# First weight loads in half units, tile order in two mixers, and gate rows made by transposes, in a twelve-step transformer kernel

## The reference

```python
def modulate(x, g, shift, scale):
    return rms_norm(x, g) * (1.0 + scale) + shift

def macaron_half_ffn(x, g, shift, scale, gate, w_in, w_out):
    return x + 0.5 * gate * swiglu_2(modulate(x, g, shift, scale), w_in, w_out)
```

## Time and profile before

| | |
|---|---|
| median of 3 runs | 3711.2 us (3710.67 to 3714.84) |
| span of the profiled execution | 3705.4 us |
| TensorE busy | 3626.4 us (98%), 18926 matmuls |
| VectorE, ScalarE, GpSimd busy | 2313.8, 1524.9, 273.7 us |
| loads by SP, and by GpSimd | 579.22 MB, 78.56 MB |
| chain that ended last, by engine | PE 91%, DVE 5%, ACT 3%, DMA 1%, issue 1% |

### The profile page before, as it was taken

How to read it: one execution, slowest core, us unless ns; L and a number is a source line. 1 busy time by engine, 2 the same in 40 slices (tenths; PEclk the granted TensorE clock), 3 DMA queues, 4 the chain that set the end, 5 groups by cost and what they waited for, 6 DMA issues and landing times.

```text
span 3705.4 us, 48300 instructions
## 1 busy us (share of the span) xinstructions
PE 3626.4 (98%) x18926; PEld 3031.7 (82%) x18926; DVE 2313.8 (62%) x3018; ACT 1524.9 (41%) x2001; POOL 273.7 (7%) x322
## 2 busy tenths in 40 slices
PE   8999999999999999999999999999999999999999
PEld 7898788889788875888898788888888588889887
DVE  6767577774577755777777576555434555555654
ACT  4454244443434424444463344444311444444443
POOL 0003200000000001000004100000000200000000
PEclk9999999999999999999999999999999999999999
DMA  9652177664476744676641384555521355454452
GB/s 317 228 160 86 59 244 242 239 216 153 165 255 204 261 147 145 236 241 224 219 160 37 120 275 167 204 170 195 175 79 53 118 179 196 170 181 155 171 185 99
DMA packets 453679, 660.58 MB, mean 178 GB/s; under 512 B 15305, under 2 KB 385444, under 8 KB 453049
## 3 DMA queue, kind: packets, MB, share of 16 engines
q1 hardware_dynamic: 431970, 579.22, 46.0%
q0 software_dynamic: 21072, 78.56, 6.6%
q10 hardware_dynamic: 454, 0.26, 0.0%
HBM read 656.94 MB, written 2.00 MB: 178 GB/s over the span
## 4 chain that ended last, share of the span: by engine, by line
PE 91%; DVE 5%; ACT 3%; issue 1%; DMA 1%; POOL 0%; ACTq 0%; SPq 0%; POOLq 0%; DVEq 0%
PE ps L813 14%; PE ps L815 14%; PE ps L814 14%; PE ps L833 7%; PE ps L835 7%; PE ps L834 7%; PE ps L3260 3%; PE ps L1160 2%; PE ps L823 2%; PE ps L1579 2%; DVE parts L750 1%; PE ps L507 1%; PE ps L509 1%; PE ps L508 1%; PE ps L3257 1%; ACT parts L736 1%
## 5 line engine op out<-in xcount | busy, mean ns | idle before, releaser
L750 DVE TENSOR_TENSOR parts<-ring,parts 128x2048 fp32r<-128x2048 f32 (+1 forms) x339 | 756.9, 2234 | 575.1 <-ACT parts L736 575.1
L813 PE MATMUL ps<-parts 128*128 128x512 f32 x2288 | 906.3, 396 | 0.5 <-DVE parts L1020 0.5
L815 PE MATMUL ps<-parts 128*128 128x512 f32 x2288 | 892.9, 390 | 0.0
L814 PE MATMUL ps<-parts 128*128 128x512 f32 x2288 | 892.0, 390 | 0.0
L736 ACT ACTIVATE parts<-ring 128x2048 fp32r<-128x2048 f32 x346 | 661.3, 1913 | 543.6 <-PE ps L815 421.4
L815 PEld LDWEIGHTS ps<-parts 128*128 128x128 f32 x2288 | 429.7, 188 | 91.0
L813 PEld LDWEIGHTS ps<-parts 128*128 128x128 f32 x2288 | 430.2, 188 | 85.9 <-issue 1.7
L814 PEld LDWEIGHTS ps<-parts 128*128 128x128 f32 x2288 | 430.5, 188 | 84.5
L833 PE MATMUL ps<-parts 128*128 128x512 f32 x1144 | 451.0, 394 | 0.7 <-DVE parts L757 0.5
L835 PE MATMUL ps<-parts 128*128 128x512 f32 x1144 | 446.6, 390 | 0.0
L834 PE MATMUL ps<-parts 128*128 128x512 f32 x1144 | 445.8, 390 | 0.0
(11 more groups left out here) (444 smaller groups left out, 4591.0 us busy)
## 6 DMA issues: line engine op xcount, KB each, us to landing
ring<-in_ffn_w_gu SPq DMA_DIRECT2D x176, 1024.0 KB
ring<-in_ffn_w_in SPq DMA_DIRECT2D x110, 1024.0 KB
ring<-in_ffn_w_down SPq DMA_DIRECT2D x88, 1024.0 KB
ring<-in_ffn_w_out SPq DMA_DIRECT2D x55, 1024.0 KB
ring<-in_gdn_w_in SPq DMA_DIRECT2D x32, 1024.0 KB
arena<-in_w_mod POOLq DMA_DIRECT2D x24, 1024.0 KB, 5.9
xn<-in_w_mod POOLq DMA_DIRECT2D x24, 1024.0 KB, 7.5
arena<-in_w_mod POOLq DMA_DIRECT2D x48, 512.0 KB, 9.0
```

Of the source, the lines that this page charges most:

```text
L750: ins = nc.vector.tensor_tensor(lower, unit_raw(at, j)[:, sides_, :], upper, ALU.subtract)
L813: nc.tensor.matmul(dst, h_u, w_u[:, :, n, :], start=(k == 0), stop=False)
L814: nc.tensor.matmul(dst, h_u, w_l[:, :, n, :], start=False, stop=False)
L815: ins = nc.tensor.matmul(dst, h_l, w_u[:, :, n, :], start=False, stop=(k == KD - 1))
```

## The change

- **First loads.** x comes in two DMAs, one for each row tile, each with its own semaphore. The gate and up weights of load 0 come as four DMAs of 0.5 MB instead of two of 1 MB: first the two that make unit 0, then the two that make unit 1, with one semaphore for each unit; the output weights raise the slot's semaphore by 48 alone. Three semaphores that were used once are shared with later uses, whose counts are raised.
- **First step.** ScalarE squares all four quarters, casts unit 0, casts the four quarters, casts unit 1. VectorE splits unit 0 ahead of the quarters of tile 0, and unit 1 ahead of `rows_dve`. TensorE's order becomes: transposes of tile 0, spin, `up(0,0,0)`, transposes of tile 1, `up(0,0,1)`, `rows_pe`, `up(0,1,0)`, `up(0,1,1)`.
- **sb and sgu.** The first four products are unit 0 tile 0, unit 1 tile 0, unit 0 tile 1, unit 1 tile 1. `unit_freed` follows: the buffer of unit 0 is free after the third product (it was the second), that of unit 1 after the fourth.
- **Gate rows.** The broadcasts in `gate_pe` and `weigh` are transposes instead of fp32 products.

```diff
@@ ffn_load
+        if it is None and g == 0:
+            for half in range(2):
+                ks = slice(half * KD // 2, (half + 1) * KD // 2)
+                for side in range(2):
+                    sp.dma_start(part(g, side).rearrange("p (k f) -> p k f", k=KD)[:, ks, :],
+                                 gu_v[:, ks, side * FF:side * FF + CH]).then_inc(first_units[half], 16)
+            sp.dma_start(part(g, 2).rearrange("p (j d) -> p j d", d=D), down_v[0]).then_inc(load_done[s], 48)
+            return
@@ unit_freed
-        first = at["kind"] in ("ffn", "gdn") and j < 2 and at is not PLACES[0]
+        first = at["kind"] in ("ffn", "gdn", "sb", "sgu") and j < 2 and at is not PLACES[0]
         return 2 * at["unit"] + (3 + j if first else 2 * j + 2)
@@ gu_upper_act
-        if j == 0 or g != unit_load(at, j - 1):
+        if at is PLACES[0] and j < GU_SLOTS:
+            act.wait_ge(first_units[j], 32)
+        elif j == 0 or g != unit_load(at, j - 1):
@@ down_upper_act
+        if g == 0 and j == 0:
+            act.wait_ge(load_done[0], 48)
@@ ffn_pe
-        early = at is PLACES[0] or at["n"] in (CTX_FFN, CTX_FFN + 1)
+        early = at["n"] in (CTX_FFN, CTX_FFN + 1)
...
-        if early:
+        if at is PLACES[0]:
+            spin(9, 3)
+        elif early:
             norm_pe(pe, at, 1)
-            if at is PLACES[0]:
-                rows_pe(pe)
-                spin(9, 3)
-            elif at["n"] == CTX_FFN:
+            if at["n"] == CTX_FFN:
...
         up(0, 0, 0)
-        if not early:
+        if at is PLACES[0] or not early:
             norm_pe(pe, at, 1)
         for half, t in ((0, 1), (1, 0), (1, 1)) if at is PLACES[0] else ((1, 0), (0, 1), (1, 1)):
             up(0, half, t)
+            if at is PLACES[0] and (half, t) == (0, 1):
+                rows_pe(pe)
@@ ffn_act
-        if at["n"] >= 8:
+        if at["n"] >= 8 or at is PLACES[0]:
             square_act(act, at, NQ - 1, 0, src)
+        if at is PLACES[0]:
+            gu_upper_act(act, at, 0)
...
         if at is PLACES[0]:
-            for j in range(GU_SLOTS):
-                gu_upper_act(act, at, j)
+            gu_upper_act(act, at, 1)
             rows_act(act)
@@ ffn_dve
         def lower_rows(t):
+            if at is PLACES[0] and t == 0:
+                gu_lower_dve(dve, at, 0)
...
         if at is PLACES[0]:
+            gu_lower_dve(dve, at, 1)
             rows_dve(dve)
-            split_first_dve(dve, at)
@@ sb_pe
+        for t in range(TT):
+            pe.wait_ge(h_split, NQ * at["split"] + 2 * t + 2)
+            for j in range(GU_SLOTS):
+                pe.wait_ge(gu_lower, at["unit"] + j + 1)
+                value_products(j, t)
+                if t == 0 and j == 0:
+                    norm_pe(pe, at, 1)
+        for j in range(GU_SLOTS, UNITS["sb"]):
...
@@ gate_pe (and the same in weigh)
-            ins = nc.tensor.matmul(ps[:, gate_bank(at) + k // 4, (k % 4) * P:(k % 4 + 1) * P], c.to_broadcast([P, P]), ident,
-                                   start=True, stop=True)
+            ins = nc.tensor.transpose(ps[:, gate_bank(at) + k // 4, (k % 4) * P:(k % 4 + 1) * P], c.to_broadcast([P, P]),
+                                      ident)
@@ sgu
-    SGU = [("v", 8 + q, t) for q in range(8) for t in range(TT)] + [("u", q, i) for q in range(8) for i in range(2)]
+    SGU = [("v", 8 + q, t) for t in range(TT) for q in range(2)] + \
+        [("v", 8 + q, t) for q in range(2, 8) for t in range(TT)] + [("u", q, i) for q in range(8) for i in range(2)]
+    def sgu_unit(n):
+        return n % 2 if n < 4 else n // 2
...
-            if n < TT:
-                pe.wait_ge(h_split, NQ * at["split"] + 2 * n + 2)
+            if n in (0, 2):
+                pe.wait_ge(h_split, NQ * at["split"] + n + 2)
@@ block.sync
-            sp.dma_start(x_sb[:, :, :], A["x"][0].rearrange("(t p) d -> p t d", p=P)).then_inc(x_loaded, 16)
+            for t in range(TT):
+                sp.dma_start(x_sb[:, t, :], A["x"][0, t * P:(t + 1) * P, :]).then_inc(x1_and_out_done if t else x_loaded, 16)
```

More of the change, by code:

```diff
@@ L235, in build @@
     a_parts = sem("a_parts")
-    out_done = sem("out_done")
+    x1_and_out_done = sem("x1_and_out_done")
     dve_step = sem("dve_step")
@@ L318, in square_act @@
             if at["kind"] == "ffn":
-                act.wait_ge(ctx_loaded, 16)
+                act.wait_ge(unit0_and_ctx_loaded, 32 + 16)
                 act.wait_ge(m_step, KD * 8 * M_FFN)
@@ L327, in square_act @@
         else:
-            act.wait_ge(x_loaded, 16)
+            act.wait_ge(*((x1_and_out_done, 16) if t else (x_loaded, 16)))
         if n:
@@ L954, in ffn_act @@
                 .then_inc(h_upper, 1)
-            if q == 0 and at["n"] < 8:
+            if q == 0 and at["n"] < 8 and at is not PLACES[0]:
                 square_act(act, at, NQ - 1)
@@ L2000, in sb_pe, with value_products @@
         mod_rest_pe(pe, at)
-        for j in range(UNITS["sb"]):
+        def value_products(j, t):
+            row_products(ps[:, 4 + 2 * t + j // 2, (j % 2) * CH:(j % 2 + 1) * CH], slice(t * P, (t + 1) * P),
+                         *unit_parts(at, j)).then_inc(up_done, 1)
+        for t in range(TT):
[6 more added lines that the diff above has]
+        for j in range(GU_SLOTS, UNITS["sb"]):
             pe.wait_ge(gu_lower, at["unit"] + j + 1)
-            w_u, w_l = unit_parts(at, j)
             for i in range(2):
                 if j < 4:
[L2007 to L2018, removed]
+                    value_products(j, i)
+                    continue
+                c = 2 * (j - 4) + i
+                if c >= 4:
+                    pe.wait_ge(sb_qks, c - 3)
+                column_products(ps[:, c % 4, 0:T], *unit_parts(at, j), slice(i * P, (i + 1) * P)).then_inc(up_done, 1)
         pe.wait_ge(sb_qks, 16)
@@ L2594, in build @@
     m_sum = sem("m_sum")
-    ctx_loaded = sem("ctx_loaded")
+    unit0_and_ctx_loaded = sem("unit0_and_ctx_loaded")
     mod_ready = sem("mod_ready")
@@ L2811, in build @@
     sg_mean = sb("sg_mean", [P, 6])
-    sgu_loaded = sem("sgu_loaded")
+    unit1_and_sgu_loaded = sem("unit1_and_sgu_loaded")
+    first_units = (unit0_and_ctx_loaded, unit1_and_sgu_loaded)
     sgu_wu = sem("sgu_wu")
@@ L2857, in sgu_pe @@
             if n == 16:
-                pe.wait_ge(sgu_loaded, 64)
+                pe.wait_ge(unit1_and_sgu_loaded, 32 + 64)
                 for h in range(2):
@@ L2862, in sgu_pe @@
                     ins.then_inc(sgu_mix, 1)
-            if i == 0:
-                pe.wait_ge(gu_lower, at["unit"] + n // 2 + 1)
+            pe.wait_ge(gu_lower, at["unit"] + sgu_unit(n) + 1)
             if n >= 4:
                 pe.wait_ge(sgu_s, n - 3)
-            w_u, w_l = unit_parts(at, n // 2)
+            w_u, w_l = unit_parts(at, sgu_unit(n))
             if side == "v":
@@ L2936, in sgu_act @@
         for n, (side, q, i) in enumerate(SGU):
-            if i == 0 and 0 < n // 2 < UNITS["sgu"] - 1:
+            if n % 2 == 0 and 0 < n // 2 < UNITS["sgu"] - 1:
                 gu_upper_act(act, at, n // 2 + 1)
@@ L2995, in scale @@
             v = sg_v[:, t, :]
-            dve.wait_ge(sgu_loaded, 64)
+            dve.wait_ge(unit1_and_sgu_loaded, 32 + 64)
             dve.wait_ge(sgu_rs, t + 2)
@@ L3317, in weigh @@
                 r = e_r[:, 8 * s + 4 * d + h:8 * s + 4 * d + h + 1]
-                nc.tensor.matmul(ps[:, 2, h * P:(h + 1) * P], r.to_broadcast([P, P]), ident, start=True, stop=True)
+                nc.tensor.transpose(ps[:, 2, h * P:(h + 1) * P], r.to_broadcast([P, P]), ident)
                 nc.tensor.matmul(ps[:, 3, h * P:(h + 1) * P], q[h], e_kT[:, h, tile * P:(tile + 1) * P],
@@ L3725, in _ @@
                 SP[at["kind"]](sp, at)
-            sp.wait_ge(out_done, 16 * TT)
+            sp.wait_ge(x1_and_out_done, 16 + 16 * TT)
         @block.scalar
```

13 lines of the change are left out of this document (7 added, 6 removed).

## The result

The changed kernel took **3715.55 us** (median of 20 runs, 3706.57 to 3723.23), the kernel before 3710.93 (20 runs, 3702.69 to 3714.84). The ratio is **1.0014**, 95% interval 1.0008 to 1.0020: slower by 0.14%, where 3706.8 had been predicted, range 3703.0 to 3712.0. The two profiled executions lie further apart: spans 3705.4 and 3714.7, +9.3 us. The profiled run of the changed kernel itself took 3716.42, 1.7 us more than its span.

A forecast was written before the change was run, and what follows sets the result against it. TensorE, busy 98% of the span, was taken as the bound, except that the start ends with load 2. Terms +0.9 - 1.0 - 1.8 - 0.6 - 0.1 - 1.8 = -4.4 gave 3706.8 us, range 3703.0 to 3712.0.

The forecast's parts named there:

- Start, +0.9: First loads and first step: load 2 issued at 25.9 instead of 18.85, a queue pause delaying `down(1)` by 0.9 us.
- so unit 0 is there at 26.54 - 14.8 = 11.8: Start: unit 0's weights land at 11.8 us, reckoned back from load 1's end at 0.355 MB a us.
- rival (b): Start: TensorE at 1.2 GHz in `up(0,0,0)`, the transposes and `up(0,0,1)`; +6.0 us, 3712.8; chance 0.10.
- Rival (a): Start: load 2 is not delayed, so the start costs 0; 3705.9 us; chance 0.15.
- Rival (e): Start: each of three added DMAs opens a gap in the queue; +4.5 us, 3711.3; chance 0.05.
- Gates -0.9, -0.9, weigh -1.8: Gate rows of ffn 8 and 9 save 0.9 us each as transposes; `weigh`'s 16 broadcasts save 1.8 in all.
- ffn 10 to 12 -0.2 each, even mixer -0.1: Gate rows elsewhere: 0.2 us saved in each of ffn 10 to 12, 0.1 in the even mixer.
- Rival (c): Gate rows and `weigh`: transposes of a broadcast column are no faster, 0.22 each; 3712.0 us; chance 0.08.
- sb 0: sb's new product order gains 1.7 us, which the later freeing of unit 0's buffer takes back: 0.
- rival (d): sb and sgu: the casts of unit 2 keep up, 1.7 us more gained in each; 3703.4; chance 0.07.
- sgu -1.0: sgu's new product order, with a gate row in it, starts unit 2's product 1.0 us sooner.
- the 5.8 us between the span and the median: Whole kernel: median 3711.2 lies 5.8 us above the profiled span 3705.4, taken as unchanged.

The follow-up runs named there:

- e11: The changed kernel plus 16 unread products between `down(0)` and `down(1)`; no run time given, in its profile load 2 lands at 45.38 us.
- e3: The changed kernel with gate rows and `weigh` as products again instead of transposes; 3715.8 us.
- e2: The changed kernel with first loads, first step and shared semaphores as in the kernel before; 3711.0 us.
- e5: e1 with every transpose of the gate rows and `weigh` issued twice; 3711.3 us.
- e1: The changed kernel with `rows_pe` right behind the transposes of row tile 0, ahead of the spin; ratio interval 0.9991 to 1.0009.

## Why the prediction was wrong, point by point

- **Start, +0.9: +3.6, and 1.6 of clock.** The first step that failed is "so unit 0 is there at 26.54 - 14.8 = 11.8". The steps from there to the end of `rows_pe` were right: forecast 8.95 us, in the trace 8.90 (19.09 to 27.99). But unit 0 landed at 14.09, and at 12.6 to 13.8 in the ten other profiles with these first loads. A mean rate tells when the bytes are through on the average; the semaphore waits for the last of its 32 signals, 16 for each of the unit's two DMAs. Of these 31 had come by 13.00 and the last at 14.09; so 1.1 of the 2.3 us is one late signal, and why the others came 1.2 behind the mean rate was not looked into. `up(0,0,0)` started 2.4 late, load 2 was issued 2.1 late (28.0, not 25.9), the hole in the queue was 3 us and not 0.9, and load 2 landed 3.6 later than before, at 46.06, past the text's own sign of being wrong ("after 45"): "every us of later issue is a us" held within 0.6.
- **What the wait does to the clock** was not a term at all. The 0.5 us of idle time ahead of `down(1)` grew to 3.9, and the clock fell for `down(1)`, which it did not with the wait filled (e11). The text had the clock as a rival in block 0's first two products only. There the matmuls took 0.23 in the changed kernel's profile, so rival (b) did not come about in it; e3's profile, with the same start, has it in part (`up(0,0,0)` at 0.43 from 18.4 to 21.8).
- **Rival (a)**, no delay: no. **Rival (e)**, with 1.5 us for each added DMA: no; from 8 to 26 us the queue, with eight weight DMAs behind one another where there had been six, moved 6.27 MB, 0.348 a us (before: 0.355). The fit of 2.0 us a DMA in the Trainium skill ("DMA: Bandwidth & Descriptors", Anatomy of one DMA) is headed there as one for DMAs that GpSimd issues, and SP issued these; by these rates it does not add up DMA by DMA in this queue.
- **Gates -0.9, -0.9, weigh -1.8**: -0.91, -0.91, -1.81. **ffn 10 to 12 -0.2 each, even mixer -0.1**: 0 in ffn 10, -0.14 in ffn 11, -0.1 in ffn 12, 0 in the even mixer. Rival (c) falls: a broadcast column is turned at the transposes' pace.
- **sb 0**: -0.4 beside the fall, -0.2 in e2; the wait for unit 2 is there (1.45, forecast 1.7), so rival (d) falls. **sgu -1.0**: -1.1.
- **The sum** was -4.4 and is -1.7 by the same terms as measured. What turned it round is the second step that failed, a term that the working put at nothing without a reason: that TensorE's clock would grant the changed kernel what it had granted before. By the means of the runs it went from 0.9935 to 0.9916, and at 2.7 us per 0.001 that is an estimated 5.1 us, about all that lies between the kernels; at one clock they are 0.3 apart (3714.1 and 3714.4), which that rough reading does not tell from -1.7.
- The comparison with the median was off as well: the 5.8 us between the span and the median were taken as a constant. The changed kernel's profiled run is 1.7 us above its own span; with the same 1.7, the profiled execution before took an estimated 3707.1 and lay some 4 us below its kernel's median. This moves no term of the sum, but it is why the two profiles lie 9.3 us apart and the medians 4.6.

## What to carry to other kernels

A load that is issued behind a signal depends on all that the signal's engine does before: when work is put ahead of such a signal, move the signal's step first, and cost a landing by its last signal, not by the mean rate. On a kernel that keeps TensorE busy for 98%, look at the granted clock stretch by stretch, in several executions, before and after: here a change that saved work lost it again through the clock, at places that it had not touched. To tell what an instruction does to the clock from what its duration does, give the time back without giving the instruction back, as e5 does.

## What the runs showed of the hardware that was not expected

- The clock fell although TensorE was busy for the whole stretch ahead of the fall: 2724.5 to 2728.1 us of the changed kernel hold 32 matmuls of 16 columns back to back, about 0.11 us apart (groups by line and shape: count | busy us, mean ns). In five of the 13 profiles the same matmuls were not followed by a fall:

```profile
L3285 PE MATMUL ps<-ring,arena 128*128 128x16 f32 x32 | 3.7, 261 | 0.0
```

- The low stretch in attention is not of one length. In e1 it lasts 23.89 us with 57 matmuls; in e5 the same 23.9 us hold 27 in the low part and 57 in the 10.25 us behind it. So a low stretch that goes on has fewer matmuls in it; that this is what lets it go on was not tried. Following the instructions through both traces, the longer stretch costs 4.2 us in e1 and e2 and 2.5 in the changed kernel.
- The spread of the kernel before from run to run goes with the clock: its 89 runs have mean clocks from 0.992 to 0.996, and about 1 us of scatter is left around the line of 2.7 us per 0.001.
